# Centring from a channel sum in PSUM, and adding output products from their PSUM banks, in the mixer of a streaming encoder step

## The reference

```python
def token_mixers(xn, ...):
    proj = einsum('bld,de->ble', xn, w_in)
    h_a, c_a, b_a, v_b, g_b = split(proj, ...)
    y_a = rmsnorm(b_a * causal_dwconv(c_a * h_a, conv_a_w), out_norm_a_g)       # 3 taps, 512 channels
    conv_out_b = causal_dwconv(v_b * sigmoid(g_b), conv_b_w)                    # 31 taps, 512 channels
    z = silu(layernorm(conv_out_b + conv_b_b, conv_norm_g, conv_norm_b))
    y_b = rmsnorm(z, out_norm_b_g)
    return einsum('ble,ed->bld', concatenate([y_a, y_b]), w_out)

def layernorm(x, g, b):
    mu = mean(x); xc = x - mu
    return xc * rsqrt(mean(xc * xc) + EPS) * g + b

h = x + token_mixers(rmsnorm(x), ...)
y = rmsnorm(h + peer(rmsnorm(h), ...))      # peer: top-k routing over 128 x 128 single-neuron experts
```

## Time and profile before

| | before |
|---|---|
| median of 3 runs | 1599.29 us (1598.38 to 1603.12) |
| the profiled execution | 1607.05 us, its span 1605.3 us |
| PE busy | 1540.7 us, 96% of the span |
| DVE busy | 1222.5 us, 76% |
| ACT busy | 651.6 us, 41% |
| POOL busy | 809.6 us, 50% |
| DMA | 407.59 MB, mean 254 GB/s |

### The profile page before, as it was taken

The page is one execution under the profiler, slowest core; times in us unless marked ns, Lnnn a source line. Parts: engine busy times, 40 slices in busy tenths (PEclk is TensorE's granted clock), DMA queues, the critical chain, the costliest instruction groups (busy, mean ns, idle before and its releaser), DMA issues.

```text
span 1605.3 us, 26947 instructions
## 1 busy us (share of the span) xinstructions
PE 1540.7 (96%) x9360; PEld 1507.0 (94%) x9360; DVE 1222.5 (76%) x2594; ACT 651.6 (41%) x841; POOL 809.6 (50%) x494
## 2 busy tenths in 40 slices
PE   7998889999999989999999998999999999999996
PEld 6997879998999989899898998999999999999996
DVE  7998984788998987787787630677777777777775
ACT  5344443343333335566565523333333333333332
POOL 5686433346667666576666775243343444344301
PEclk9999989999999999999999999999999999999999
DMA  4221212227667767999999997789999898999841
GB/s 177 93 79 57 79 66 80 79 95 248 227 225 271 252 219 275 341 375 364 348 345 343 359 398 258 240 328 353 343 341 336 331 330 320 350 345 345 326 165 56
DMA packets 150078, 407.59 MB, mean 254 GB/s; under 512 B 12288, under 2 KB 76032, under 8 KB 148224
## 3 DMA queue, kind: packets, MB, share of 16 engines
q1 hardware_dynamic: 90208, 215.11, 39.5%
q0 software_dynamic: 36864, 134.23, 22.1%
q10 hardware_dynamic: 22944, 57.58, 9.2%
HBM read 349.99 MB, written 56.89 MB: 253 GB/s over the span
## 4 chain that ended last, share of the span: by engine, by line
PE 86%; DVE 6%; DMA 5%; ACT 2%; issue 1%; POOL 0%; SPq 0%; another core or an unknown queue 0%; ACTq 0%; DVEq 0%
PE ps_unit L760 32%; PE ps_unit L820 18%; PE ps_misc L820 18%; PE ps_unit L564 12%; PE ps_misc L794 3%; DMA acts_dram<-act_ring 3%; DMA raw<-stream 2%; PE ps_misc L720 1%; PE ps_unit L652 1%; DVE mov_lo L1162 1%; DVE sq L1170 1%; ACT gates L1073 1%; DVE hid L1278 1%; PE ps_unit L707 0%; DMA rows<-u_rows,expert 0%
## 5 line engine op out<-in xcount | busy, mean ns | idle before, releaser
L446 POOL TENSOR_TENSOR w_lo<-raw,w_hi 128x1024 fp32r<-128x1024 f32 x172 | 417.8, 2433 | 314.8 <-ACT w_hi L875 190.2
L760 PE MATMUL ps_unit<-mov_hi,w_hi 128*128 128x416 f32 x1024 | 367.6, 359 | 9.9 <-POOL w_lo L446 9.9
L528 POOL DMA_INDIRECT rows<-v_rows,expert x128 | 207.0, 1617 | 318.8 <-DVE sums L1366 310.0
L760 PE MATMUL ps_unit<-mov_hi,w_lo 128*128 128x416 f32 x1024 | 363.4, 355 | 0.0
L760 PE MATMUL ps_unit<-mov_lo,w_hi 128*128 128x416 f32 x1024 | 360.9, 352 | 0.0
L875 ACT ACTIVATE w_hi<-raw 128x1024 fp32r<-128x1024 f32 x300 | 315.7, 1053 | 87.8 <-ACT act_ring L1045 56.8
L1097 ACT ACTIVATE prod_hi<-prod 128x416 fp32r<-128x416 f32 x128 | 70.7, 552 | 369.5 <-PE ps_misc L820 368.2
L760 PEld LDWEIGHTS ps_unit<-mov_hi,w_hi 128*128 128x128 f32 x1024 | 194.7, 190 | 13.2 <-ACT w_hi L875 6.6
L1552 DVE TENSOR_TENSOR prod_lo<-prod,prod_hi 128x416 fp32r<-128x416 f32 x128 | 75.7, 592 | 171.0 <-ACT prod_hi L1097 170.1
L760 PEld LDWEIGHTS ps_unit<-mov_lo,w_hi 128*128 128x128 f32 x1024 | 195.0, 190 | 2.7
L760 PEld LDWEIGHTS ps_unit<-mov_hi,w_lo 128*128 128x128 f32 x1024 | 194.4, 190 | 1.7
(11 more groups left out here) (218 smaller groups left out, 2736.2 us busy)
## 6 DMA issues: line engine op xcount, KB each, us to landing
raw<-stream SPq DMA_DIRECT2D x300, 512.0 KB
acts_dram<-act_ring ACTq DMA_DIRECT2D x128, 208.0 KB
gates_dram<-gates ACTq DMA_DIRECT2D x13, 2048.0 KB
gates_in<-gates_dram SPq DMA_DIRECT2D x16, 1664.0 KB, 14.7
acts_in<-acts_dram SPq DMA_DIRECT2D x32, 832.0 KB, 7.3
hid<-x_t SPq DMA_DIRECT2D x8, 272.0 KB, 5.9
rows<-u_rows,expert POOLq DMA_INDIRECT x128
rows<-v_rows,expert POOLq DMA_INDIRECT x128
```

The lines of the kernel that those rows point to most:

```text
L446: nc.gpsimd.tensor_tensor(w_lo[:, j, :], raw[:, j, :], w_hi[:, j, :].bitcast(F32), ALU.subtract).then_inc(lo_made, 1)
L528: nc.gpsimd.indirect_dma_start(out=rows[:, n % ROWS_RING, :], out_offset=None, in_=table, in_offset=bass.IndirectOffsetOnAxis(ap=expert[:, ...
L760: last = nc.tensor.matmul(dense_psum(j), w[:, j, k * P:(k + 1) * P], m[:, k, 0:DENSE], start=(k == 0 and n == 0), stop=(k == KC - 1 and n ...
```

## The change

Two places on VectorE, and the waits that go with them. The mean is no longer written to SBUF: each of the four chunks is centred by one scalar_tensor_tensor that reads the channel sum in PSUM, multiplies it by -1/512 and adds the chunk. In add_output the product with 1/rms is written back to the output's own PSUM banks, and the add reads it there; dve_took is raised by the add in place of the product, so TensorE gets the banks after the add. ScalarE's squares of hid wait on dve_took instead of hid_made, and hid_made counts only the late halves.

```diff
--- before.py
+++ after.py
@@ -974,11 +974,11 @@
                 if n in (2, 4):
                     split_high(FIRST_Q // RING, n // 2 - 1)
                 if n < KC - 2:
-                    act.wait_ge(hid_made, n + 1)
+                    act.wait_ge(dve_took, KC + n + 1)
                     nc.scalar.activation(sq[:, n], hid[:, n], ACT.Square).then_inc(sq_made, 1)
             for a in range(2):
                 for n in (KC - 2, KC - 1):
-                    act.wait_ge(hid_made, n + 2 * a + 1)
+                    act.wait_ge(hid_made, n - (KC - 2) + 2 * a + 1)
                     nc.scalar.activation(half(sq[:, n], a), half(hid[:, n], a), ACT.Square).then_inc(sq_made, 1)
             act.wait_ge(rstd_made, 4)
             for a in range(2):
@@ -1241,11 +1241,9 @@
                 mov_low(KC + c, c, proj[:, 2 * WC + 3 * c], par_col("out_a_g", c))
 
             dve.wait_ge(sum_done, 2)
-            mean = conv[:, 0:T]
-            step(nc.vector.tensor_scalar(halves(mean), sum_psum(0), 1.0 / WIDTH, None, ALU.mult))
-            settle()
             for c in range(WC):
-                nc.vector.tensor_tensor(proj[:, 2 * c], proj[:, 2 * c], mean, ALU.subtract).then_inc(centred, 1)
+                nc.vector.scalar_tensor_tensor(out=halves(proj[:, 2 * c]), in0=sum_psum(0), scalar=-1.0 / WIDTH,
+                                               in1=halves(proj[:, 2 * c]), op0=ALU.mult, op1=ALU.add).then_inc(centred, 1)
             for c in range(1, WC - 1):
                 dve.wait_ge(sq_made, SQ_X + c + 1)
                 ins = nc.vector.tensor_tensor(sq[:, WC], sq[:, WC], sq[:, WC + c], ALU.add)
@@ -1273,13 +1271,10 @@
                 else:
                     dve.wait_ge(out_half_done, q // 2 + 1)
                 k = q % KC
-                nc.vector.tensor_tensor(halves(part[q % 2]), out_psum(q), halves(factor), ALU.mult).then_inc(dve_took, 1)
-                dve.wait_ge(dve_took, q + 1)
-                ins = nc.vector.tensor_tensor(hid[:, k], hid[:, k], part[q % 2], ALU.add)
-                if q < KC:
-                    step(ins)
-                else:
-                    ins.then_inc(hid_made, 1)
+                step(nc.vector.tensor_tensor(out_psum(q), out_psum(q), halves(factor), ALU.mult))
+                settle()
+                dve.wait_ge(dve_took, q)
+                nc.vector.tensor_tensor(halves(hid[:, k]), halves(hid[:, k]), out_psum(q), ALU.add).then_inc(dve_took, 1)
 
             reciprocal(2, rstd[:])
             dve.wait_ge(rstd_made, 2)
@@ -1322,7 +1317,7 @@
                 dve.wait_ge(sq_made, SQ_H + KC - 1 + 2 * a)
                 nc.vector.tensor_tensor(half(sq[:, 0], a), half(sq[:, 0], a), half(sq[:, KC - 2], a),
                                         ALU.add).then_inc(sq_added, 1)
-            dve.wait_ge(hid_made, KC + 2)
+            dve.wait_ge(hid_made, 4)
 
             for a in range(2):
                 dve.wait_ge(std_made, 5 + a)
```

## The result

| | before | changed |
|---|---|---|
| median | 1600.66 us (6 runs, 1598.38 to 1603.12) | 1591.53 us (6 runs, 1588.46 to 1595.41) |
| profiled execution | 1607.05 us, span 1605.3 | 1588.46 us, span 1586.6 |
| ratio | 1 | 0.994, 95% interval 0.9924 to 0.9955 |

The account below looks back on a forecast made before the run. TensorE was taken as the bound (86% of the chain), VectorE mattering only within a 49 us stretch. Gains 3.0 + 5.2 + 2.2 - 0.6 + 0.7 = 10.5 us, from 1599.3 to 1588.8 us; range 1585.0 to 1596.5.

Parts of the forecast that it names:

- part 1: Centring from PSUM, ahead of the root: root 3.0 us earlier, between 2.0 and 4.4 by TensorE's clock.
- tail: Adds of the last outputs no longer held by GpSimd: 0.7 us gained, 0 in the worst case.
- The hold: VectorE instructions with both inputs in SBUF wait until the GpSimd instruction they meet ends; PSUM-input forms are spared, about 0.72 us.
- forms held as well: Rival: the new PSUM forms are held too, only the 0.7 us mean copy is gained, 1598.6 us; chance 0.07.
- Six outputs: Output 0's product to the first low part: 11.3 us undisturbed becomes 8.3; capped by TensorE, 2.7 us less.
- hand-over: Banks return to TensorE after the add, 0.75 us later; hidden except at output 10, costing 0.6 us.
- Low parts and gap: Low parts finish about when the GpSimd split at 178.52 starts; TensorE starts output 8 at 181.2 instead of 186.41, 5.2 us.
- Clock: Without the idle time before output 8, TensorE's half clock behind it, about 4.5 us long, goes too: 2.2 us.
- Lost later: Rival: DMA writes and loads of later stages swallow half the gain, 1594 us; chance 0.12.
- Bank hand-over as a loser: Rival: adds stay held, outputs 4 to 13 each get banks 0.75 us later, 6.8 us slower, 1606; chance 0.05.

Follow-up runs that it names:

- e1: Kernel before with only the centring from PSUM, output products and adds through SBUF as before: ratio 0.9987, stage 104.33 us against 108.43 before.
- e5: Changed kernel with products kept in PSUM banks only for outputs 8 to 13, earlier outputs through SBUF: stage 105.55 us (98.30 changed), 14.22 to the root.
- e4: Changed kernel with products kept in PSUM banks only for outputs 0 to 7, later outputs through SBUF: stage 96.88 us (98.30 changed), 11.83 to the root.
- e3: Changed kernel with the scaled mean an instruction again, written in PSUM and read there by four subtractions: stage 99.82 us against 98.30 changed.
- e6: Changed kernel with one more 3.54 us reciprocal into an unread buffer ahead of the four low parts: stage 105.88 us against 98.30 changed.
- e2: Kernel before with only the output adds reading products from PSUM banks, mean copy and SBUF subtractions as before: ratio 0.9959, stage 101.97 us.
- e8: Changed kernel with group b's reciprocal root also in PSUM, where four products read it: ratio 0.9926, stage 97.83 us against 98.30 changed.
- e9: e8 with three of output 0's four channel chunks (18 matmuls) multiplied ahead of the sum of squares: ratio 0.9913, stage 95.05 us.
- e10: Changed kernel run again unchanged, on one chip with e11: median 1591.30 us, ratio 0.994, stage 98.12 us.
- e11: e9 run again unchanged, on the same chip as e10: median 1586.52 us, ratio 0.9916, stage 95.05 us.

## Why the prediction was right, point by point

The forecast was 1588.8 us, 10.5 less than before; measured 1591.5 and 9.1 to 9.6 less, with 10.1 in the stage. The sum counted from a median of 1599.3, which with more runs is 1600.7; that is 1.4 of the 2.7 us between 1588.8 and 1591.5. In the trace the terms come to 3.6 for part 1, 4.6 up to output 8, 2.1 for the clock, -0.8 at output 10 and 0.6 for the tail, 10.1 together. The mechanism is the predicted one. That the sum came so close is partly luck: part 1, where I had taken the middle between two ends by the clock, gave 0.6 more than that, and the rest 1.0 less.

- **Part 1, 3.0 us.** Measured 3.6 at the root, by e1 3.5. The steps cost 0.71, not 0.73. The open question in this step, whether the clock falls behind 4 us of idle time, has no single answer: seven times it did, once it didn't. My ends of 2.0 and 4.4 hold what was seen in e5 (2.4) and miss e4 (4.8) by 0.4. That at full clock ScalarE's table load would be last, as I had it, is what e4 shows.
- **The hold.** The reading of rows 5 carried the sum, and e3 confirms it by the operand's place, with the instructions kept. The rival "forms held as well" is out. The Trainium skill, in SBUF — State Buffer, section Who interferes with whom, says that a VectorE instruction with at most one SBUF input, outside its two-port modes, does not contend with GpSimd; the new forms agree at 0.706 to 0.733 us, those inside splits among them. The Trainium skill, in VectorE: DVE Perf Modes, section Rules for kernel authors, offers for work on a matmul result either to read PSUM at single rate or to copy it to SBUF first if many operations follow; the copy would have lost here: the four SBUF reads took 5.49 us and the four PSUM reads 2.60.
- **Six outputs, 2.7 us.** Measured 1.97: 167.12 to 178.43 is 11.31 us before, 163.25 to 172.59 is 9.34 now. The step that was mis-sized is TensorE's. I let the bank hand-over count at output 10 only; at output 4 it costs too, because output 0's add waits for the reciprocals while TensorE is already through output 3. TensorE stopped there (0.34 us of idle time in the rows) and started output 4 14.2 us behind the root where it had been 13.7, so output 5 came 0.5 us later and VectorE idled 0.86 before it. The other 0.2 us are in my own sum, which let output 5's product start at 174.1, before TensorE was through with it at 174.3.
- **Low parts and gap, 5.2 us.** From the root to output 8 it was 31.8 us before and is 27.2 now, so 4.6; the missing 0.6 is that same late start of output 4, since TensorE runs through from there. The low parts fit ahead of the split at 175.23 as worked out: the four take 2.87 us from 172.59, so the last began some 0.5 us before the split (0.4 was forecast). e6 shows what a miss costs.
- **Clock, 2.2 us; hand-over, 0.6; tail, 0.7.** From output 8 to the key scoring 60.0 us became 58.1: 1.9 together, where I had 2.3. Before, outputs 8 and 9 took 8.13 us, 2.1 above full clock; so the clock's 2.2 is right. The hand-over at output 10 cost 0.8, 0.65 of it idle time. Behind output 10 another 0.6 was gained. There VectorE did better than I had it, for output 10's product came 5.9 us earlier relative to the root and output 13's 6.9; but the last late product came only 6.4 earlier, since TensorE's second late half (L683) waits for output 13's add. That loss was named as the worst case and was the case. In e4, where the product hands over but adds are held again, the same instruction waits 0.56 us for the product instead.
- **Carried to the end.** The medians give 9.1 to 9.6 of the stage's 10.1, and their interval takes in 10.1. The other kernels with several runs agree: by their ratios e1 gains 2.1, e2 6.6, e8 11.9, e9 13.9, e10 9.6 and e11 13.4 us, where one trace of each has a stage shorter by 4.1, 6.5, 10.6, 13.4, 10.3 and 13.4. With the changed kernel that is 67 us for 68. "Lost later" isn't supported, nor excluded for a half microsecond.
- **Bank hand-over as a loser.** Excluded in this kernel: it costs 0.5 us at output 4, 0.8 at output 10 and some 0.5 at the late halves, since elsewhere TensorE's 3.04 us per output covers VectorE's 1.5.

What stays open: why the clock stayed at full in e4 alone behind the same idle time, and what makes the later piece of the program vary by 13 us from one execution to the next.

## What to carry to other kernels

Where VectorE and GpSimd work side by side, look at the spread of one VectorE line, not its mean: a line whose longest is three times its shortest, with both inputs in SBUF, may be held, and GpSimd's instructions in order of time beside it decide. Leaving one operand in PSUM freed it here, at about 0.02 us per product written back. Check what that does to the bank: it cost only where TensorE already had to wait for VectorE's next output. And an idle stretch of TensorE on the way to a root is worth filling with early matmuls, for the work and for the clock (e9).

## What the hardware showed that I hadn't expected

- The price of a delay isn't proportional to it. 3.54 us more work ahead of the low parts cost 7.7 us, twice that cost 9.3, because the first delay made them meet two splits (6.33 us for four) and the second only one (4.73).
- GpSimd loses by some meetings too: three sums of squares took 5.47 us beside SBUF adds, 4.25 beside PSUM adds, and the splits that began while a VectorE instruction with two SBUF inputs was running took 2.71 to 2.93 us (145.56, 173.68, 178.52 and 204.78 before). Splits that were running when it came kept their 2.34 to 2.47, such as that of 175.59 in e6 (2.38), which held a low part.
- The same 24 float32 matmuls behind the same 3.86 us of idle time took 5.97 to 8.52 us, by when the granted clock changed, which alone moved the root by 2.4 us between executions with the same code up to there.
